# Moving the RMSNorm factor of a two-layer decoder trunk behind its matmuls

## The reference

```python
def rmsnorm(x, g):
    y = xf * lax.rsqrt(jnp.mean(xf * xf, axis=-1, keepdims=True) + EPS)
    return (y * g).astype(x.dtype)

def trunk_layer(h, p_i, ...):
    z = rmsnorm(h, norm_mix) @ w_in
    ...                       # pooling mixer, Conformer convolution, short convolution
    h = h + jnp.concatenate([y_a, y_b, y_c], axis=-1) @ w_out
    up = rmsnorm(h, norm_ffn) @ w_up                          # 2048 -> 2 x 5632
    upc, new_ffn = causal_dwconv(st_ffn, up, ffn_conv)        # width 3, per channel
    h = h + (silu(upc[..., :D_FF]) * upc[..., D_FF:]) @ w_down
    gate = sigmoid(rmsnorm(h, norm_ple) @ ple_gate)
    h = h + (p_i @ ple_proj) * gate
```

## Time and profile before

| | |
|---|---|
| median shown, two runs | 3781.41 us |
| profiled execution | 3552.99 us |
| its span, first to last instruction, slowest core | 3551.4 us |
| spans of the 8 cores | 3531.5 to 3551.4 us |
| mean granted TensorE clock, slowest core | 0.960 |
| TensorE busy | 3298.8 us (93%) |
| VectorE busy | 1581.4 us (45%) |
| ScalarE busy | 930.8 us (26%) |
| DMA | 466.37 MB, mean 131 GB/s |

### The profile page before, as it was taken

How to read it: one execution, slowest core, us unless ns; L and a number is a source line. 1 busy time by engine, 2 the same in 40 slices (tenths; PEclk the granted TensorE clock), 3 DMA queues, 4 the chain that set the end, 5 groups by cost and what they waited for, 6 DMA issues and landing times.

```text
span 3551.4 us, 69512 instructions; the slowest of 8 cores (3531.5 to 3551.4 us)
## 1 busy us (share of the span) xinstructions
PE 3298.8 (93%) x27952; PEld 2752.7 (78%) x27952; DVE 1581.4 (45%) x2859; ACT 930.8 (26%) x1434; POOL 484.2 (14%) x914
## 2 busy tenths in 40 slices
PE   7998999988998999998599999999789989999987
PEld 5886888877887888887478778888667877888865
DVE  3334454433433444443254264564335426456443
ACT  2222232232122322332212232232221223223222
POOL 0111111111011111111001111111110111111110
PEclk9999999998999999999799999999999999999988
DMA  7587999975467999986746778889864678888975
GB/s 138 96 133 120 142 146 155 143 128 100 72 109 126 151 148 146 141 144 111 194 85 111 129 132 142 136 143 151 202 100 72 108 126 141 143 137 140 152 151 110
DMA packets 149436, 466.37 MB, mean 131 GB/s; under 512 B 21760, under 2 KB 26624, under 8 KB 148096
## 3 DMA queue, kind: packets, MB, share of 16 engines
q0 software_dynamic: 133856, 425.83, 73.7%
q1 hardware_dynamic: 15264, 36.10, 3.0%
HBM read 869.70 MB, written 17.94 MB: 250 GB/s over the span
## 4 chain that ended last, share of the span: by engine, by line
PE 85%; DVE 6%; DMA 4%; ACT 2%; issue 2%; DVEq 0%; SPq 0%; ACTq 0%; POOL 0%; POOLq 0%
PE ps L125 85%; DVE xn L125 4%; DMA wb<-w_up 2%; DVE U L125 1%; DMA h<-xT 1%; ACT U L125 1%; DMA wb<-w_down 1%; ACT rstd L125 1%; DMA wb<-w_out 0%; ACT L125 0%; DVE cat L125 0%; ACT xn L125 0%; DVE h L125 0%; ACT cat L125 0%; DVEq L121 0%
## 5 line engine op out<-in xcount | busy, mean ns | idle before, releaser
L125 PE MATMUL ps<-xn,wb 128*128 128x264 bf16 (+1 forms) x17664 | 2105.7, 282 | 102.5 <-DVE xn L125 80.0
L125 PEld LDWEIGHTS ps<-xn,wb 128*128 128x128 bf16 x17664 | 1738.2, 99 | 452.4 <-issue 145.4
L125 DVE SCALAR_TENSOR_TENSOR U<-U,cstt 128x528 f32<-128x528 f32 x752 | 577.9, 768 | 549.6 <-ACT U L125 509.6
L125 ACT ACTIVATE U<-ps 128x528 f32<-128x528 f32 (+1 forms) x484 | 298.6, 617 | 1636.2 <-PE ps L125 1220.6
L125 PE MATMUL ps<-U,wb 128*128 128x264 bf16 (+1 forms) x5920 | 694.0, 281 | 30.0 <-DVE U L125 21.1
L125 PEld LDWEIGHTS ps<-U,wb 128*128 128x128 bf16 x5920 | 583.7, 99 | 137.7 <-issue 32.9
L125 DVE TENSOR_TENSOR h<-ps,h 128x528 f32<-128x528 f32 (+1 forms) x320 | 228.5, 716 | 665.3 <-PE ps L125 665.3
L125 POOL DMA_DIRECT2D wb<-w_up x352 | 186.1, 529 | 1008.8 <-PE ps L125 985.0
L125 ACT ACTIVATE U<-ps,cstt 128x528 f32<-128x528 f32 (+1 forms) x376 | 263.7, 701 | 128.4 <-PE ps L125 128.4
L125 PE MATMUL ps<-cat,wb 128*128 128x264 bf16 (+1 forms) x2048 | 236.0, 279 | 9.2 <-DMA wb<-w_out 6.1
L125 DVE TENSOR_TENSOR U<-ps,U 128x528 f32<-128x528 f32 (+1 forms) x112 | 80.2, 716 | 363.2 <-ACT U L125 363.2
(11 more groups left out here) (49 smaller groups left out, 748.7 us busy)
## 6 DMA issues: line engine op xcount, KB each, us to landing
wb<-w_up POOLq DMA_DIRECT2D x352, 512.0 KB, 6.9
wb<-w_down POOLq DMA_DIRECT2D x256, 352.0 KB, 5.6
wb<-w_in POOLq DMA_DIRECT2D x136, 512.0 KB, 6.0
wb<-w_out POOLq DMA_DIRECT2D x64, 512.0 KB, 8.0
wb<-ple_gate POOLq DMA_DIRECT2D x64, 512.0 KB, 5.9
h<-xT SPq DMA_DIRECT2D x8, 1056.0 KB, 14.2
wb<-conf_pw POOLq DMA_DIRECT2D x24, 192.0 KB, 3.6
yT<-xn SPq DMA_DIRECT2D x2, 2112.0 KB, 7.4
```

What stands on the lines that cost most here:

```text
L125: ins = getattr(e, name)(*a, **kw)
```

## The change

Both norms of the FFN and of the PLE gate are split. In the loop ahead of each, where `h` gets its last addend, ScalarE now also writes `xn_t` = h * gain, without the factor (`xnp_chunk`), and the squares go to another place: at the FFN norm to the top of the arena (`sqtop`, an added barrier for ScalarE and VectorE at m = 0 guards it), at the PLE norm to `cat_t`. After the barrier, which stays, `rmsnorm_stats` makes the statistics and `rstd_t` and nothing more. The factor is applied to what comes out of w_up and ple_gate, by a VectorE multiply out of PSUM. In the FFN that multiply writes `raw`, and ScalarE makes `acc` from `raw` instead of from PSUM; ScalarE's copy falls away. In PLE it writes `gs`, and the Sigmoid works in place there. The norms ahead of w_in and at the end are unchanged.

```diff
+                def xnp_chunk(m, gname, l):
+                    g = cs(gname, l * 16 + m)
+                    S.op("act", (lambda e: e.activation(out=xn_t[:, m, 0:W], in_=h_t[:, m, 0:W], func=AF.Identity, scale=g)),
+                         reads=[hB[m], B["cst"]], writes=[xnB[m // 2]])
+
+                def rmsnorm_stats(region):
...
+                    slot = mm_job(KC, (lambda k: ones_t[:]), (lambda k: sqv[:, k, 0:W]), [B["ones"]], kreads=[(0, 14, early), (14, 16, bf(14))])
+                    S.op("act", (lambda e: e.activation(out=v2(rstd_t[:, 0:W]), in_=psv(slot), func=AF.Ln, scale=1.0 / D, bias=EPS)),
+                         reads=[psb[slot]], writes=[B["rstd"]])
+                    S.op("act", (lambda e: e.activation(out=rstd_t[:, 0:W], in_=rstd_t[:, 0:W], func=AF.Exp, scale=-0.5)), reads=[B["rstd"]], writes=[B["rstd"]])
...
                         slot = linear(w_out, l * KC + m, KC, cat_t, B["cat"])
+                        if m == 0:
+                            S.barrier(("act", "dve"))
...
-                        sq_chunk(m, "xn")
+                        xnp_chunk(m, "nffn", l)
+                        sq_chunk(m, "top")
 
                     S.barrier()
-                    rmsnorm("nffn", l, "xn", presq=True)
+                    rmsnorm_stats("top")
...
                             if q == FC // GS - 1:
-                                sq_chunk(m, "xn")
+                                xnp_chunk(m, "nple", l)
+                                sq_chunk(m, "cat")
...
                                 s_ = linear(w_up, l * 2 * FC + ab * FC + j, KC, xn_t, "xn")
-                                S.op("act", (lambda e: e.activation(out=v2(raw[:, ab, 2:2 + W]), in_=psv(s_), func=AF.Copy)),
-                                     reads=[psb[s_]], writes=[rawB[i2][ab]])
-                                S.op("act", (lambda e: e.activation(out=v2(acc[:, ab, 0:W]), in_=psv(s_), func=AF.Identity,
+                                S.op("dve", (lambda e: e.tensor_tensor(out=v2(raw[:, ab, 2:2 + W]), in0=psv(s_), in1=v2(rstd_t[:, 0:W]), op=ALU.mult)),
+                                     reads=[psb[s_], B["rstd"]], writes=[rawB[i2][ab]])
+                                S.op("act", (lambda e: e.activation(out=acc[:, ab, 0:W], in_=raw[:, ab, 2:2 + W], func=AF.Identity,
                                                                     scale=cst_t[:, wo + 3 * ab + 2:wo + 3 * ab + 3])),
-                                     reads=[psb[s_], B["cst"]], writes=[accB[i2][ab]])
+                                     reads=[rawB[i2][ab], B["cst"]], writes=[accB[i2][ab]])
...
-                    rmsnorm("nple", l, "xn", presq=True)
+                    rmsnorm_stats("cat")
...
                         sg_ = linear(ple_gate, l * KC + m, KC, xn_t, "xn")
-                        S.op("act", (lambda e, sg_=sg_, i2=i2: e.activation(out=v2(gs_a[i2][:, 0:W]), in_=psv(sg_), func=AF.Sigmoid)), reads=[psb[sg_]], writes=[gsB[i2]])
+                        S.op("dve", (lambda e, sg_=sg_, i2=i2: e.tensor_tensor(out=v2(gs_a[i2][:, 0:W]), in0=psv(sg_), in1=v2(rstd_t[:, 0:W]), op=ALU.mult)),
+                             reads=[psb[sg_], B["rstd"]], writes=[gsB[i2]])
+                        S.op("act", (lambda e, i2=i2: e.activation(out=gs_a[i2][:, 0:W], in_=gs_a[i2][:, 0:W], func=AF.Sigmoid)), reads=[gsB[i2]], writes=[gsB[i2]])
```

More of the change, by code:

```diff
@@ L248, in program @@
                                            ("cst", "s_cst"), ("ptw", "s_ptw"), ("carry", None), ("ost0", "s_ost0"), ("ost1", "s_ost1"),
-                                           ("zero", None), ("ones", None), ("onesf", None), ("warm", None), ("stp", "s_stp"), ("stc", "s_stc"), ("sts", "s_sts"),
+                                           ("zero", None), ("ones", None), ("onesf", None), ("warm", None), ("sqtop", None), ("stp", "s_stp"), ("stc", "s_stc"), ("sts", "s_sts"),
                                            ("stf", "s_stf"), ("rstd", None)]}
@@ L255, in program @@
             st = {"psj": 0, "fresh_xn": False}
+            sqtop_v = U_t[:, NU - KC * WMAX // 2:NU].bitcast(BF16).rearrange("p (k w) -> p k w", k=KC)
             yv0 = xn_t[:].rearrange("p k w -> p (k w)").bitcast(F32).rearrange("p (k w) -> p k w", k=8)
@@ L308, in sq_region @@
                         return xn_t, (lambda k: [xnB[k // 2]])
+                    if region == "top":
+                        return sqtop_v, (lambda k: [B["sqtop"]])
                     return cat_t, (lambda k: [B["cat"]])
+                def xnp_chunk(m, gname, l):
[3 more added lines that the diff above has]
+                def rmsnorm_stats(region):
+                    sqv, bf = sq_region(region)
+                    early = []
+                    for k in range(0, 14, 2):
+                        early += bf(k)
+                    slot = mm_job(KC, (lambda k: ones_t[:]), (lambda k: sqv[:, k, 0:W]), [B["ones"]], kreads=[(0, 14, early), (14, 16, bf(14))])
+                    S.op("act", (lambda e: e.activation(out=v2(rstd_t[:, 0:W]), in_=psv(slot), func=AF.Ln, scale=1.0 / D, bias=EPS)),
+                         reads=[psb[slot]], writes=[B["rstd"]])
+                    S.op("act", (lambda e: e.activation(out=rstd_t[:, 0:W], in_=rstd_t[:, 0:W], func=AF.Exp, scale=-0.5)), reads=[B["rstd"]], writes=[B["rstd"]])
                 def warm_lnexp():
```

## The result

The changed kernel is slower: the ratio to the kernel before is 1.0128, 95% interval 1.0108 to 1.0149, medians of all runs 3601.82 us (11) and 3555.83 us (10). The profiled execution took 3598.49 us, the one before 3552.99: 45.5 us more, where the sum of the prediction gave 34.

What follows compares the result with a forecast made beforehand. TensorE was taken as the bound, idling at the norms, with VectorE close behind in the FFN; gains of 107.8 us and costs of 141.9 us took 3553 us to 3587 us, range 3540 to 3665 us (forecast's own 3545 to 3625).

Steps and rivals of the forecast that it cites:

- the sum of the prediction: Whole kernel: gains of 107.8 us at the norms against costs of 141.9 us, net +34 us.
- the forecast of no change: Whole kernel: VectorE bounds the FFN of pass 1, losses and gains nearly cancel; within 2% put at 0.74.
- Removed at the norms: FFN and PLE norms: TensorE goes on without waiting for scaled copies; gains of 54.6 us and 53.2 us.
- Gap: Ahead of FFN and PLE statistics: one more ScalarE operation, 1.86 us becomes 2.5; costs 5.2 us, plus 12 for clock.
- VectorE's cycle: FFN, per j, including waits for ScalarE: 8.99 us against TensorE's 7.41 in pass 1, 7.35 against 7.20 in pass 0.
- Waits at the down_proj: FFN of pass 1: TensorE waits for the tail of each group's last j; 51.8 us per layer, 103.6 in all.
- Clock after the waits: Down_proj in pass 1: slower matmuls after three more waits per layer, 2.2 us each, 13.2 us in all.
- Rival 1: FFN of pass 1: short waits for PSUM pairs make TensorE's clock oscillate; total 3666 us, chance 0.17.
- Rival 2: FFN: PSUM's lead hides VectorE's wait, so the FFN costs nothing; total 3470 us, chance 0.05.
- Rival 3: FFN of pass 0: weight loads set the pace, so the norm's 26.2 us gain is lost; 3613 us, chance 0.08.

Runs made afterwards that it cites:

- the runs on the gap: Changed kernel with TensorE out of the FFN and PLE barriers, square before gain copy: 1.0090; later, best kernel so far (0.971) with squares named by pair: 0.9620.
- the reordered kernel: Changed kernel with the VectorE multiplies of both halves ahead of the taps of both in each FFN step: ratio 0.9779, median 3480.94 us.
- both edits together: Changed kernel with both multiplies ahead of the taps, TensorE out of the FFN and PLE barriers, and square before gain copy: ratio 0.9744, about 3464 us.

## Why the prediction was right or wrong

**What failed is the forecast of no change, at the size of what a measurement can tell.** The sum gave +34 us, about 1%. The prediction took 2% (71 us) as the least that a measurement of this kernel can tell, so it put "within 2%" at 0.74 and slower at 0.20. That 2% had no row behind it. Measured is 1.28% with an interval of 0.2% to either side, so a sum of +1% should have been put as slower. In the sum itself the mechanism, the place and the sign were right. The term that was mis-sized most is the waits ahead of the down_proj in pass 1, put at 103.6 us; by the same count they measured 115.

**By stretches**, from the start of one statistics to the next, profiled executions (the sum's terms laid out on the stretches where they fall):

| stretch | sum of the prediction | measured |
|---|---|---|
| FFN, pass 0, two layers | 2 x -9.2 | -11.2, -8.6 |
| FFN, pass 1, two layers | 2 x +46.4 | +55.4, +50.9 |
| PLE, four | 4 x -10.7 | -11.1, -10.9, -10.9, -11.8 |
| elsewhere (in the sum: the longer gaps ahead of the FFN statistics) | +2.6 | +3.7 |
| all (spans) | +34 | +45.6 |

**Removed at the norms: right.** Pass 0 and PLE gained what the sum gave within 2 us per stretch. The step after the statistics came off as described: w_up goes on at once, and in pass 0 TensorE stops after four jobs. The fifth starts 17.0 us after the statistics at layer 0 and 15.8 us at layer 1, 15.9 expected. The profile names the weights for the stop at layer 1 and VectorE for the one at layer 0; but the multiply that frees the fifth job's PSUM pair had ended 12 us earlier, so there too it is likely the weights.

**Gap: right in length, its cause only half seen.** 2.49 us instead of 1.86 in pass 0, 2.53 instead of 1.89 in pass 1. Six of the eight statistics ran slow, 5.4 or 5.5 us for 3.8, some 10 us in all where I took 12. That "the barrier stays" holds TensorE was wrong in part, as the runs on the gap showed: the single name did as well.

**VectorE's cycle: right.** 9.05 us measured, 8.99 from pieces of another stage; 7.40 in pass 0 (from multiply to multiply, 705.63 to 713.02 us) for 7.35.

**Waits at the down_proj: under-sized.** Start of w_up to first down_proj 112.67 us for 111.5; the next two 94.9 and 95.35 for 93.6; the last 86.67 for 85.2. That is 5.7 us more in layer 0, and the same in layer 1. The cycle's 0.06 us explains 41 x 0.06 = 2.5 of it. Another 2.2 us are seven steps of layer 0 that took 9.20 to 9.42 us instead of 9.05, for a reason that the trace doesn't show; the last 1.0 us stays open. The last down_proj of layer 0 took 58.6 us for 55.1 before, with waits for weights, a term that the sum did not have. Together they are the miss of pass 1, 13.5 us: 2 x 5.7 + 3.5 = 14.9, less the 1.5 us counted for the slow statistics of layer 1, which didn't come.

**Clock after the waits: right.** The inner down_proj took 42.0 to 43.6 us for 40.8, 2.2 us more on average, as I took it.

**Rival 1, the clock oscillating in the FFN of pass 1, did not happen.** The window with one stop of 1.24 us per step in the changed kernel (columns as in the earlier trace rows):

```profile
2071.00:2106.00 35.00, 30.83 (x256) 24.47 (x256) 24.35 (x54) 8.17 (x12) 3.71 (x7) 1.00 0.63 105
2106.00:2115.00 9.00, 0.10 (x1) 0.00 (x0) 6.30 (x15) 2.04 (x3) 0.53 (x1) 0.79 0.29 45
2115.00:2120.00 5.00, 4.51 (x28) 3.32 (x29) 3.23 (x8) 0.75 (x1) 0.00 (x0) 0.69 0.00 0
```

The granted clock is 1.00 (2.4 GHz) through the short stops and falls only in the long one, which is paid in the next few us. The Trainium skill's "TensorE: Matmul & The Clock Gate", section "A second HAM failure mode: psum-queue depth-cycling", describes such an oscillation for short idles between bursts; this case's trace has the cycling for PSUM pairs, with 12% idle, and not the oscillation.

**Rival 2** (the wait hidden) would have been 3470 us. It did not happen in the change, but the reordered kernel is much like this rival made true, at 3481. **Rival 3** (weights): no, pass 0 kept its gain. Two slips of the prediction change nothing: (9 x 0.15 + 0.4) x 2 is 3.5 us and not 3.6, and the slow start of 2.5 us in rival 1 is called the largest bound, which was 2.9.

## What to carry to other kernels

Taking a factor out of an operand and putting it behind the matmul moves work from a burst at a barrier to the steady state; what decides is the cycle of the in-order engine that gets it, with its waits for others in the middle, against the matmul engine's. Add up that cycle from starts of instructions in the trace (ends and busy shares hide the waits: VectorE was busy 49% of the span, and 70% in the window 2071 to 2106 us above, where it was the bound), and if it is over, first look for work to put into the wait: the same instructions in another order turned +1.3% into -2.2%. Where a consumer takes a tile in pieces, its dependence has to be named in pieces too, or the next wait stands where the removed barrier was.

## What the runs showed that I had not expected

Before the change gaps of TensorE of 1.86 or 1.89 us were followed by statistics at full clock at all eight places (3.76 or 3.87 us); in the changed kernel gaps of 2.49 or 2.53 us were followed by slow ones (5.43 or 5.54 us) at six of eight. Counted over the profiled executions of all kernels but that with both edits together, 33 gaps of 1.86 to 1.98 us had no slow statistics behind them, and of 37 gaps of 2.48 to 2.58 us 26 had. So some 0.6 us more of gap went, more often than not, with 1.7 us more in the matmuls behind it. Why it did not at the other 11 places is open.

In the changed kernel waits of 9.38 or 9.73 us ahead of an inner down_proj made it 1.3 to 2.8 us longer; the wait of 5.76 us ahead of the last one, before the change, cost its first 110 matmuls 2.2 us.
